# Two-layer streaming encoder step on one core: norm tiles, key transposes and a residual addition issued at other places

## Chip, cores and metric

One NeuronCore of a Trainium2 chip runs the whole program in one launch. The time is device microseconds of that core; the figure compared is the median over executions.

## What is computed

A step of a two-layer encoder in fp32 for 512 prompt tokens and 8 x 16 sample tokens, together 640 tokens in T = 5 tiles of 128. Each layer is mixer, cross-attention into 256 memory tokens, gated MLP, each behind an RMSNorm and followed by a residual addition:

```python
for l in range(2):
    x = x + mixer_l(rmsnorm(x, ln_mix[l]))        # l=0: attention + retention, l=1: gated linear attention
    mn = rmsnorm(mem, ln_mem[l])                  # 256 memory tokens of the prompt
    k, v = mn @ w_ck[l], mn @ w_cv[l]             # sample tokens use cached k, v, one pair per sequence
    x = x + softmax((rmsnorm(x, ln_cross[l]) @ w_cq[l]) k^T / 16) v @ w_co[l]
    x = x + conv_ffn(rmsnorm(x, ln_ffn[l]))       # gelu(conv(h Wg)) * (h Wu) @ Wdown
y = rmsnorm(x, ln_final)
```

The model width is 1024, cross-attention has 4 heads of 256. New keys, values and states are outputs too.

## The kernel before, in words

**Products.** Every large product is split into high and low fp32r parts and made of three matmuls a slice of 128 contraction rows: high x low, low x high, high x high (`three`, L784 to L788). Weights come in units of 1024 columns: SyncE loads them into `raw`, ScalarE copies out the high part (`split_hi`, L1530), VectorE subtracts to get the low part (`split_lo`, L2056). There are 5 slots for split units; ScalarE may fill one only when TensorE has marked it free, and TensorE waits for the low part. A product of one token tile by 512 columns is 8 slices, 24 matmuls of 512 columns (`proj_tile`, `proj_out`). A product with the weights standing (`cols_tile`) has two parts of 384 and 256 tokens; `cols_pair` does two such column tiles for the first three token tiles, and then both for the last two.

**Norm tiles.** For tile t of a norm, ScalarE squares and sums (L1575), GpSimd makes the reciprocal root (L535, L536), VectorE scales into `xn` (`scaled`, L2073; two buffers), TensorE transposes in two halves of four 128x128 blocks (`norm_tile`, L801 to L810), ScalarE copies the high part of each half (`halves`, L1591) and VectorE makes the low part (`halves`, L2090), which also drains the bank. These transposes, the key transposes and the scores share 3 PSUM banks in turn (`aux`); product outputs share the other 5 (`lin`). A bank can be opened again only when what was in it is drained.

**Order.** The order of each engine's work is written out by hand; every engine works its own list strictly in order and waits on semaphores. `norm_behind` (L1132) runs the last product of a stage tile by tile with the norm's transposes behind it. Its last two tiles, T-2 and T-1, are transposed inside the first product of the next chunk: `cols_pair` calls them before slice 0 and slice 3 of its second column tile (L1139).

**The parts that the change touches.** `rest(l)` holds the cross-attention and MLP of layer l, on each engine. On TensorE: query chunk `("cq", l, 0)` ends with column tiles 2 and 3, with both memory norm tiles transposed between them (L1145 to L1147); the four tiles of `("cq", l, 1)`; then the two key chunks, each of two products (memory tiles m = 0, 1), and after both products the transposes of both results (`mkT`, L1152 to L1158), for which ScalarE must have copied the product out to `mk` (L1780). VectorE copies each `mkT` block out (L2378). Then 4 of 8 slices of a value product, a wait for the last `mkT` copy, and eight score steps (`x_scores`). After the prompt's attention come NB + 3 = 11 stages s for the 8 sample sequences (L1215 to L1270): in each, part of an output product `("co", l, 0)` (`CROSS_FILL`, L186: tile 0 in stages 1 and 2, tile 1 in 3 and 4, tile 2 in 6 and 7, tile 3 in 8 and 9), transposes of the cached keys (L1227) whose copies to `kTX` ScalarE (L1814) and VectorE (L2403) share, transposes of the probabilities of sequence s - 2 (L1234), scores of sequence s - 1 (L1253), values of s - 2 (L1264). VectorE adds a finished output tile to x with `add_x` (L2104), which also drains the product's bank; in a stage it does so last (L2421).

In the MLP's down products (`down`, L2430 on VectorE) each token tile has two halves n of 512 columns. In the last group of layer 0 (`behind`) VectorE interleaves the additions with `scaled` and `halves` of norm `mix1`, and splits unit 0 of the next chunk `("in1", 0)` ahead of the addition (t, n) = (1, 0) (L2438).

Of the kernel before, what the change touches and what calls it, by code (L numbers as in the profile page):

```python
# [19 lines left out]
P = 128  # L20
D = 1024
KT = D // P
# [3 lines left out]
T = TP + 1  # L26
# [175 lines left out]
def build(nc, io, known):  # L202
# [8 lines left out]
    with ctx:  # L211
# [571 lines left out]
        def _(pe):  # L783
# [345 lines left out]
                        ins.then_inc(*unit_free.mark(c, k // 2))  # L1129
                ins.then_inc(*lin_full.mark(c, t))  # L1130

            def norm_behind(nm, product, following):  # L1132

                for t in range(T):
                    product(t)
                    if 0 < t < T - 1:
                        norm_tile(nm, t - 1)

                cols_pair(nm, following, 0, {(1, 0): lambda: norm_tile(nm, T - 2), (1, 3): lambda: norm_tile(nm, T - 1)})  # L1139
                cols_pair(nm, following, 1)  # L1140


            def rest(l):
                c = ("cq", l, 0)
                cols_tile(c, f"cross{l}", P * 2, 2)  # L1145
                norm(f"mem{l}")
                cols_tile(c, f"cross{l}", P * 3, 3, last=True)  # L1147
                for i in range(4):
                    cols_tile(("cq", l, 1), f"cross{l}", P * i, i, last=i == 3)
                for c in (("ck", l, 0), ("ck", l, 1)):  # L1150
                    proj_rows(c, f"mem{l}", 2, memT_lo, memT_hi)
                    for m in range(2):  # L1152
                        pe.wait_ge(*act_done.at("mk", l, m, c[2]))
                        out = aux.open(pe, "mkT", l, c[2], m)
                        for i in range(4):
                            k = 4 * c[2] + i
                            ins = pe.transpose(out[:, P * i:P * i + P], mk[:, m, P * k:P * k + P], ident[:, :])
                        ins.then_inc(*aux_full.mark("mkT", l, c[2], m))  # L1158

                pe.wait_ge(*act_done.at("cq", l, 1, 3))  # L1160
                pairs = [(t, hp) for t in range(TP) for hp in range(2)]

                def x_scores(t, hp):
                    out = aux.open(pe, "sX", l, t, hp)
                    for hh in range(2):
                        for dk in range(2):
                            k = 4 * hp + 2 * hh + dk
                            ins = pe.matmul(out[:, MEM * hh:MEM * hh + MEM], qT[:, t, k, :], mkT[:, k, :], start=dk == 0, stop=dk == 1)  # L1168
                    ins.then_inc(*aux_full.mark("sX", l, t, hp))
# [13 lines left out]
                        ins.then_inc(*lin_full.mark(c, m))  # L1183

                value_part(0, 0, 0)
                pe.wait_ge(*dve_done.at("mkT", l, 1, 1))
                x_scores(0, 0)
                for n, (t, hp) in enumerate(pairs):
                    if n + 1 < len(pairs):
# [130 lines left out]
                        ins = pe.transpose(out[0:18, P * (f - 4 * n):P * (f - 4 * n) + P], tailc[:, f, :], ident[:, :])  # L1320
                    ins.then_inc(*aux_full.mark("rows", l, n))
                if l == 0:
                    norm_behind("mix1", lambda t: down(GROUPS - 1, t), [(("in1", 0), 0, 0), (("in1", 0), P, 1)])
                else:
                    for t in range(T):
                        down(GROUPS - 1, t)
# [179 lines left out]
        def _(act):  # L1506
# [253 lines left out]
            def rest(l):  # L1760
                for half in range(2):
                    c = ("cq", l, half)
                    for i in range(4):
                        if i == 1:
                            split_hi(NEXT[c], [0])
                        if i == 3:
                            split_hi(NEXT[c], [1, 2, 3])
                        k = 4 * half + i
                        evac_cols(c, i, qT[:, :, k, :], 1.0, ("cq", l, half, i))
                        if half == 0 and i == 1:  # L1770
                            norm(f"mem{l}", "mem")

                def memory(name, half, m):

# [260 lines left out]
        def _(dve):  # L2035
# [332 lines left out]

            def rest(l):
                split_lo(NEXT[("cq", l, 0)], [0])  # L2370
                norm(f"mem{l}")
                split_lo(NEXT[("cq", l, 0)], [1, 2, 3])
                split_lo(NEXT[("cq", l, 1)], range(4))
                for half in range(2):
                    split_lo(NEXT[("ck", l, half)], range(4))
# [21 lines left out]
                for s in range(NB + 3):  # L2397
                    if s == 0:
                        dve.wait_ge(*put["mv"].at(l))
                    if s < NB:  # L2400
                        for n in (1, 3):
                            dve.wait_ge(*aux_full.at("kTX", l, s, n))
                            dve.tensor_copy(kTX[s % 2][:, 2 * n:2 * n + 2, :], aux.bank("kTX", l, s, n)[:, :].rearrange("p (k m) -> p k m", k=2)).then_inc(*aux_v.mark("kTX", l, s, n))  # L2403
                            dve_done.after("kTX", l, s, n)
                    if 1 <= s <= NB:
                        b, i = s - 1, (s - 1) % 2
                        dve.wait_ge(*aux_full.at("sXs", l, b))
                        link(dve.tensor_reduce(small[:, i, 0:1], aux.bank("sXs", l, b)[:, 0:MEM], AX.X, ALU.max))
                        dve.tensor_scalar(small[:, i, 1:2], small[:, i, 0:1], -1.0 / 16.0, None, ALU.mult).then_inc(*dve_done.mark("negXs", l, b))
                        dve.wait_ge(*aux_a.at("sXs", l, b))  # L2410
                        link(dve.reciprocal(small[:, i, 3:4], small[:, i, 2:3]))
                        dve.tensor_scalar(pS[:, i, :], pS[:, i, :], small[:, i, 3:4], lam_mask[:, i:i + 1], ALU.mult, ALU.mult).then_inc(*dve_done.mark("pS", l, b))
                    if s >= 4 and s % 2 == 0:
                        p = s // 2 - 2
                        dve.wait_ge(*act_done.at("oX", l, p))
                        cols = slice(SEQ + 32 * p, SEQ + 32 * p + 32)
                        dve.tensor_tensor(hT_lo[:, :, cols].rearrange("p (h j) q -> p h j q", j=2), lin.bank("oXT", l, p)[:, 0:2 * P].rearrange("p (j h q) -> p h j q", j=2, h=H),
                                          flat(hT_hi[:, :, cols]).rearrange("p (h j) q -> p h j q", j=2), ALU.subtract).then_inc(*lin_v.mark("oXT", l, p))
                    if s == NB:
                        split_lo(("co", l, 1), [0])  # L2420
                    if s in CROSS_FILL and CROSS_FILL[s][2] == KT:  # L2421
                        add_x(("co", l, 0), CROSS_FILL[s][0], 0)
                    if s == NB + 1:
                        add_x(("co", l, 0), TP - 1, 0)
                dve_done.after("oX", l)
# [4 lines left out]
                def down(g):  # L2430
# [4 lines left out]
                    for t in range(T):  # L2435
                        for n in range(2):
                            if c in NEXT:
                                if t == 1 and n == 0:  # L2438
                                    split_lo(NEXT[c], [0])
                                if t == T - 1 and n == (1 if behind else 0):  # L2440
                                    split_lo(NEXT[c], [1, 2, 3])
# [4 lines left out]
                            if behind and t and n == 0:  # L2446

                                if t < T - 1:
                                    scaled(nm, t - 1)
                                if t > 1:  # L2450
                                    halves(nm, t - 2)
                    if behind:
                        scaled(nm, T - 2)
                        scaled(nm, T - 1)
# [270 lines left out]
```

## Time and profile before

| | us |
|---|---|
| median of 3 runs | 2092.57 |
| lowest and highest of them | 2091.99, 2093.45 |
| the profiled execution | 2091.57 |
| its span in the trace | 2089.8 |
| TensorE busy, share of the span | 98% |
| VectorE / ScalarE / GpSimd busy | 47% / 36% / 10% |

The span runs from the first to the last instruction of the profiled execution; its own time is 1.8 us longer. A timeline line reads: start in us, duration in us, engine (PE TensorE, DVE VectorE, ACT ScalarE, POOL GpSimd, SP SyncE), line of the kernel, operation, out<-in by the program's names, shapes, count; in brackets the idle time of the engine before it and what ended that. Lines with a count merge instructions that follow one another.

### The profile page before, as it was taken

How to read it: one execution, taken by the hardware profiler on the slowest of the kernel's cores; microseconds unless marked ns; L12 is line 12 of the kernel's file. 1: busy time of each engine (PE TensorE's matmuls, PEld its weight loads, DVE VectorE, ACT ScalarE, POOL GpSimd, SP SyncE). 2: the span in 40 equal slices, each digit the busy share in tenths (PEclk: the TensorE clock that was granted, in tenths of full speed). 3: DMA queues.
4: the chain of work that ended last, by engine and by line, in shares of the span. 5: the costliest groups of instructions: out<-in, count | busy, mean ns of one | idle time of the engine just before them, and what ended most of it. 6: DMA issues, size and time to landing. Idle time of an engine off the chain costs nothing.

```text
span 2089.8 us, 30525 instructions
## 1 busy us (share of the span) xinstructions
PE 2040.5 (98%) x12370; PEld 1795.0 (86%) x12370; DVE 981.9 (47%) x1651; ACT 762.3 (36%) x1318; POOL 199.1 (10%) x457
## 2 busy tenths in 40 slices
PE   8999989999999999999999999999999999999997
PEld 6889667987789999999989888799778999999996
DVE  5453664435454443434453467653444444434443
ACT  4222552435344332232233446243533433223232
POOL 3012121000100000000010123210010000000000
PEclk9999999999999999999999999999999999999999
DMA  5324143235722222222221211723572132122221
GB/s 164 132 77 149 51 160 128 85 121 198 262 84 77 66 81 81 69 76 68 81 77 61 81 44 43 257 71 121 184 290 85 62 100 80 63 70 81 81 81 55
DMA packets 111066, 219.42 MB, mean 105 GB/s; under 512 B 7011, under 2 KB 52367, under 8 KB 110862
## 3 DMA queue, kind: packets, MB, share of 16 engines
q1 hardware_dynamic: 91234, 148.00, 20.8%
q0 software_dynamic: 19696, 69.47, 9.7%
q8 instruction: 102, 1.67, 0.3%
q14 instruction: 34, 0.28, 0.0%
HBM read 200.51 MB, written 18.24 MB: 105 GB/s over the span
## 4 chain that ended last, share of the span: by engine, by line
PE 93%; DVE 3%; ACT 2%; issue 1%; DMA 1%; POOL 0%; DVEq 0%; SPq 0%; ACTq 0%; POOLq 0%
PE bank L786 15%; PE bank L788 14%; PE bank L787 14%; PE bank L847 7%; PE bank L851 7%; PE bank L849 7%; PE bank L850 5%; PE bank L848 5%; PE bank L852 5%; PE bank L809 1%; PE bank L1211 1%; PE bank L1227 1%; PE bank L1168 1%; PE bank L1253 1%; PE bank L1264 1%
## 5 line engine op out<-in xcount | busy, mean ns | idle before, releaser
L2056 DVE TENSOR_TENSOR w_lo<-raw,w_hi 128x1024 fp32r<-128x1024 f32 x265 | 319.0, 1219 | 524.2 <-ACT w_hi L1530 520.3
L1530 ACT ACTIVATE w_hi<-raw 128x1024 fp32r<-128x1024 f32 x265 | 274.4, 1052 | 252.3 <-PE bank L788 202.4
L786 PE MATMUL bank<-w_hi,hT_lo 128*128 128x512 f32 x720 | 291.3, 405 | 10.4 <-DVE x L2104 4.3
L847 PE MATMUL bank<-hT_hi,w_lo 128*128 128x384 f32 (+1 forms) x856 | 290.0, 339 | 0.0
L849 PE MATMUL bank<-hT_lo,w_hi 128*128 128x384 f32 (+1 forms) x856 | 289.3, 338 | 0.0
L851 PE MATMUL bank<-hT_hi,w_hi 128*128 128x384 f32 (+1 forms) x856 | 289.3, 338 | 0.0
L788 PE MATMUL bank<-w_hi,hT_hi 128*128 128x512 f32 x720 | 282.7, 393 | 0.0
L787 PE MATMUL bank<-w_lo,hT_hi 128*128 128x512 f32 x720 | 282.1, 392 | 0.0
L848 PE MATMUL bank<-hT_hi,w_lo 128*128 128x256 f32 (+1 forms) x856 | 239.0, 279 | 0.0
L850 PE MATMUL bank<-hT_lo,w_hi 128*128 128x256 f32 (+1 forms) x856 | 239.0, 279 | 0.0
L852 PE MATMUL bank<-hT_hi,w_hi 128*128 128x256 f32 (+1 forms) x856 | 239.0, 279 | 0.0
L786 PEld LDWEIGHTS bank<-w_hi,hT_lo 128*128 128x128 f32 x720 | 136.1, 189 | 50.5 <-issue 9.4
L2104 DVE TENSOR_TENSOR x<-x,bank 128x512 f32<-128x512 f32 x160 | 109.5, 685 | 145.4 <-PE bank L788 144.6
L786 PE MATMUL bank<-w_hi,a_lo 128*128 128x512 f32 x440 | 171.7, 390 | 0.0
L788 PE MATMUL bank<-w_hi,a_hi 128*128 128x512 f32 x440 | 171.2, 389 | 0.0
L787 PE MATMUL bank<-w_lo,a_hi 128*128 128x512 f32 x440 | 171.2, 389 | 0.0
L847 PEld LDWEIGHTS bank<-hT_hi,w_lo 128*128 128x128 f32 (+1 forms) x856 | 160.0, 187 | 1.9 <-DVE memT_lo L2090 0.4
L788 PEld LDWEIGHTS bank<-w_hi,hT_hi 128*128 128x128 f32 x720 | 136.0, 189 | 29.6
L851 PEld LDWEIGHTS bank<-hT_hi,w_hi 128*128 128x128 f32 (+1 forms) x856 | 160.0, 187 | 0.6
L849 PEld LDWEIGHTS bank<-hT_lo,w_hi 128*128 128x128 f32 (+1 forms) x856 | 160.0, 187 | 0.6
L848 PEld LDWEIGHTS bank<-hT_hi,w_lo 128*128 128x128 f32 (+1 forms) x856 | 160.1, 187 | 0.5
L850 PEld LDWEIGHTS bank<-hT_lo,w_hi 128*128 128x128 f32 (+1 forms) x856 | 160.1, 187 | 0.2
(368 smaller groups left out, 2990.7 us busy)
## 6 DMA issues: line engine op xcount, KB each, us to landing
raw<-w_ffn_gate SPq DMA_DIRECT2D x44, 512.0 KB, 3.8
raw<-w_ffn_up SPq DMA_DIRECT2D x44, 512.0 KB, 4.8
raw<-w_ffn_down SPq DMA_DIRECT2D x22, 1024.0 KB, 4.8
kcX<-cache_mem_k POOLq DMA_DIRECT2D x16, 1024.0 KB, 6.6
vcX<-cache_mem_v POOLq DMA_DIRECT2D x16, 1024.0 KB, 6.9
raw<-w_in_even SPq DMA_DIRECT2D x13, 1024.0 KB, 5.3
raw<-w_in_odd SPq DMA_DIRECT2D x12, 1024.0 KB, 5.1
raw<-w_cq SPq DMA_DIRECT2D x8, 1024.0 KB, 7.3
```

What stands on the lines that cost most here:

```text
L786: pe.matmul(out, wl, xh, start=first, stop=False)
L787: pe.matmul(out, wh, xl, start=False, stop=False)
L788: return pe.matmul(out, wh, xh, start=False, stop=last)
L847: pe.matmul(oa, wl, hT_hi[:, k, 0:HA], start=f, stop=False)
L848: pe.matmul(ob, wl, hT_hi[:, k, HA:TOK], start=f, stop=False)
L849: pe.matmul(oa, wh, hT_lo[:, k, 0:HA], start=False, stop=False)
L850: pe.matmul(ob, wh, hT_lo[:, k, HA:TOK], start=False, stop=False)
L851: ia = pe.matmul(oa, wh, hT_hi[:, k, 0:HA], start=False, stop=l)
L852: ib = pe.matmul(ob, wh, hT_hi[:, k, HA:TOK], start=False, stop=l)
L1530: act.activation(w_hi[:, g % W_SLOTS, 0:n], raw[:, q % 2, UNIT * i:UNIT * i + n], ACT.Copy).then_inc(*hi_made.mark(c, u))
L2056: dve.tensor_tensor(w_lo[:, s, 0:n], raw[:, q % 2, UNIT * i:UNIT * i + n], flat(w_hi[:, s, 0:n]), ALU.subtract).then_inc(*lo_made.mark(c, u))
L2104: ins = dve.tensor_tensor(xs, xs, lin.bank(c, t, *key)[:, :], ALU.add)
```

## The change

All edits are of order; every transpose, product, copy, split and addition is there before and after, and one wait moves.

- `mix1` only: tiles T-2 and T-1 are transposed before slices 2 and 4 of the second column tile, not 0 and 3. On VectorE the split of unit 0 of `("in1", 0)` moves from before the addition (1, 0) to behind the addition (1, 1).
- The memory norm's tile 0 is transposed between query column tiles 2 and 3, tile 1 after tile 3. ScalarE makes the second tile's high part, and VectorE its low part, that much later, behind the splits of the next units.
- The key transposes go one by one: (half 0, m 0) before slice 6 of the product (0, 1), (0, 1) inside product (1, 0), (1, 0) inside product (1, 1), and (1, 1) after the first half of the value product. The score steps of token tile 0 wait for the copy of their own half's second block.
- In the stages that end an output tile (2, 4 and 7) VectorE adds it first, before the key copies.

```diff
 # TensorE
-            def norm_behind(nm, product, following):
+            def norm_behind(nm, product, following, turns=(0, 3)):
...
-                cols_pair(nm, following, 0, {(1, 0): lambda: norm_tile(nm, T - 2), (1, 3): lambda: norm_tile(nm, T - 1)})
+                cols_pair(nm, following, 0, {(1, turns[0]): lambda: norm_tile(nm, T - 2), (1, turns[1]): lambda: norm_tile(nm, T - 1)})
...
-                norm(f"mem{l}")
+                norm_tile(f"mem{l}", 0)
                 cols_tile(c, f"cross{l}", P * 3, 3, last=True)
+                norm_tile(f"mem{l}", 1)
...
-                for c in (("ck", l, 0), ("ck", l, 1)):
-                    proj_rows(c, f"mem{l}", 2, memT_lo, memT_hi)
-                    for m in range(2):
...
+                proj_tile(("ck", l, 0), f"mem{l}", 0, 2, memT_lo, memT_hi)
+                proj_tile(("ck", l, 0), f"mem{l}", 1, 2, memT_lo, memT_hi, lambda: turn_keys(0, 0))
+                proj_tile(("ck", l, 1), f"mem{l}", 0, 2, memT_lo, memT_hi, lambda: turn_keys(0, 1))
+                proj_tile(("ck", l, 1), f"mem{l}", 1, 2, memT_lo, memT_hi, lambda: turn_keys(1, 0))
...
                 def x_scores(t, hp):
+                    if t == 0:
+                        pe.wait_ge(*dve_done.at("mkT", l, hp, 1))
...
                 value_part(0, 0, 0)
-                pe.wait_ge(*dve_done.at("mkT", l, 1, 1))
+                turn_keys(1, 1)
                 x_scores(0, 0)
...
-                    norm_behind("mix1", lambda t: down(GROUPS - 1, t), [(("in1", 0), 0, 0), (("in1", 0), P, 1)])
+                    norm_behind("mix1", lambda t: down(GROUPS - 1, t), [(("in1", 0), 0, 0), (("in1", 0), P, 1)], (2, 4))
 # ScalarE
                         if half == 0 and i == 1:
-                            norm(f"mem{l}", "mem")
+                            square(f"mem{l}", "mem", 0)
+                            square(f"mem{l}", "mem", 1)
+                            halves(f"mem{l}", 0)
+                        if half == 0 and i == 3:
+                            halves(f"mem{l}", 1)
 # VectorE
                 split_lo(NEXT[("cq", l, 0)], [0])
-                norm(f"mem{l}")
+                scaled(f"mem{l}", 0)
+                scaled(f"mem{l}", 1)
+                halves(f"mem{l}", 0)
                 split_lo(NEXT[("cq", l, 0)], [1, 2, 3])
+                halves(f"mem{l}", 1)
...
                 for s in range(NB + 3):
                     if s == 0:
                         dve.wait_ge(*put["mv"].at(l))
+                    if s in CROSS_FILL and CROSS_FILL[s][2] == KT:
+                        add_x(("co", l, 0), CROSS_FILL[s][0], 0)
...
-                    if s in CROSS_FILL and CROSS_FILL[s][2] == KT:
-                        add_x(("co", l, 0), CROSS_FILL[s][0], 0)
...
-                                if t == 1 and n == 0:
+                                if t == 1 and n == 0 and not behind:
                                     split_lo(NEXT[c], [0])
...
+                            if behind and (t, n) == (1, 1):
+                                split_lo(NEXT[c], [0])
```

## Rows read from the trace of the kernel before

**Rows 1.** The page: busy time by engine, share of the span, instructions

```profile
PE 2040.5 (98%) x12370; PEld 1795.0 (86%) x12370; DVE 981.9 (47%) x1651; ACT 762.3 (36%) x1318; POOL 199.1 (10%) x457
```

**Rows 2.** Who waited for whom, TensorE: us in total, times, longest us

```profile
PE bank L786 <- DVE x L2104: 4.3, 3, 1.9
...
PE bank L809 <- DVE memT_lo L2090: 1.1, 2, 0.5
```

**Rows 3.** Timeline, down products of layer 0, first transposes of norm mix1

```profile
1062.34 1.23 DVE L2056 TENSOR_TENSOR w_lo<-raw,w_hi 128x1024 fp32r<-128x1024 f32 x1 [2.24 <-ACT w_hi L1530]
...
1064.20 1.28 DVE L2073 SCALAR_TENSOR_TENSOR xn<-x,rstd,gain 128x1024 f32<-128x1024 f32 x1
...
1064.36 0.39 PE L788 MATMUL bank<-w_hi,a_hi 128*128 128x512 f32 x1
...
1065.54 0.66 PE L809 MATMUL bank<-ident,xn 128*128 128x128 f32 x4 [0.79 <-DVE xn L2073]
```

**Rows 4.** Timeline, column pair behind it, tiles T-2 and T-1 of norm mix1

```profile
1088.76 0.34 PE L788 MATMUL bank<-hT_hi,w_hi 128*128 128x384 f32 x1
1089.78 1.06 PE L809 MATMUL bank<-ident,xn 128*128 128x128 f32 x8 [0.68 <-DVE xn L2073]
...
1090.33 1.29 DVE L2073 SCALAR_TENSOR_TENSOR xn<-x,rstd,gain 128x1024 f32<-128x1024 f32 x1 [0.81 <-POOL rstd L536]
...
1092.27 1.03 PE L809 MATMUL bank<-ident,xn 128*128 128x128 f32 x8
...
1093.53 1.29 DVE L2090 TENSOR_TENSOR hT_lo<-bank,hT_hi 128x512 fp32r<-128x512 f32 x2 [0.72 <-ACT hT_hi L1591]
```

**Rows 5.** Timeline, a norm tile without a wait, then the two memory tiles, layer 0

```profile
384.70 1.04 PE L809 MATMUL bank<-ident,xn 128*128 128x128 f32 x8
...
385.50 0.42 PE L786 MATMUL bank<-hT_hi,w_lo 128*128 128x384 f32 x1
...
403.80 1.47 PE L809 MATMUL bank<-ident,xn 128*128 128x128 f32 x12
...
406.44 0.41 PE L847 MATMUL bank<-hT_hi,w_lo 128*128 128x384 f32 x1
```

**Rows 6.** Timeline, TensorE, first block of key transposes of layer 0

```profile
452.63 0.60 PE L1157 MATMUL bank<-ident,mk 128*128 128x128 f32 x4
...
453.89 0.47 PE L786 MATMUL bank<-w_hi,memT_lo 128*128 128x512 f32 x1
454.20 0.39 PE L787 MATMUL bank<-w_lo,memT_hi 128*128 128x512 f32 x1
454.43 0.39 PE L788 MATMUL bank<-w_hi,memT_hi 128*128 128x512 f32 x1
```

**Rows 7.** Timeline, key transposes to scores, stages 3 and 5, layer 0

```profile
536.88 1.94 PE L1227 MATMUL bank<-ident,kcX 128*128 128x128 f32 x16
...
538.97 1.07 PE L1253 MATMUL bank<-kTX,qT 128*32 128x256 f32 x16
...
547.87 2.00 PE L1227 MATMUL bank<-ident,kcX 128*128 128x128 f32 x16
...
549.45 0.67 DVE L2104 TENSOR_TENSOR x<-x,bank 128x512 f32<-128x512 f32 x1
...
550.99 1.07 PE L1253 MATMUL bank<-kTX,qT 128*32 128x256 f32 x16 [0.32 <-DVE kTX L2403]
```

**Rows 8.** Timeline, stage 7 and the product of stage 8, layer 0; last, layer 1

```profile
562.78 1.94 PE L1227 MATMUL bank<-ident,kcX 128*128 128x128 f32 x16
...
563.86 0.69 DVE L2403 COPY kTX<-bank 128x512 f32<-128x512 f32 x1 [2.39 <-PE bank L1227]
...
568.72 0.50 PE L786 MATMUL bank<-w_hi,hT_lo 128*128 128x512 f32 x1 [1.91 <-DVE x L2104]
...
1567.26 0.50 PE L786 MATMUL bank<-w_hi,hT_lo 128*128 128x512 f32 x1 [1.78 <-DVE x L2104]
```

**Rows 9.** Stretches: length, busy of PE PEld DVE ACT POOL, granted clock, DMA share, GB/s

```profile
519.00:552.00 33.00, 32.29 (x288) 24.52 (x290) 16.81 (x34) 12.02 (x27) 6.42 (x9) 1.00 0.85 312
```

More of the change, by code:

```diff
@@ L1145, in rest, with turn_keys @@
                 cols_tile(c, f"cross{l}", P * 2, 2)
-                norm(f"mem{l}")
+                norm_tile(f"mem{l}", 0)
                 cols_tile(c, f"cross{l}", P * 3, 3, last=True)
+                norm_tile(f"mem{l}", 1)
                 for i in range(4):
                     cols_tile(("cq", l, 1), f"cross{l}", P * i, i, last=i == 3)
-                for c in (("ck", l, 0), ("ck", l, 1)):
-                    proj_rows(c, f"mem{l}", 2, memT_lo, memT_hi)
-                    for m in range(2):
[L1153 to L1158, printed above, removed]
+                def turn_keys(half, m):
+                    pe.wait_ge(*act_done.at("mk", l, m, half))
+                    out = aux.open(pe, "mkT", l, half, m)
+                    for i in range(4):
+                        k = 4 * half + i
+                        ins = pe.transpose(out[:, P * i:P * i + P], mk[:, m, P * k:P * k + P], ident[:, :])
+                    ins.then_inc(*aux_full.mark("mkT", l, half, m))
+                proj_tile(("ck", l, 0), f"mem{l}", 0, 2, memT_lo, memT_hi)
+                proj_tile(("ck", l, 0), f"mem{l}", 1, 2, memT_lo, memT_hi, lambda: turn_keys(0, 0))
+                proj_tile(("ck", l, 1), f"mem{l}", 0, 2, memT_lo, memT_hi, lambda: turn_keys(0, 1))
+                proj_tile(("ck", l, 1), f"mem{l}", 1, 2, memT_lo, memT_hi, lambda: turn_keys(1, 0))
                 pe.wait_ge(*act_done.at("cq", l, 1, 3))
```

## The prediction

> **What bounds the kernel now.** I read the page first, then the list of who waited for whom, then the timeline around each wait of TensorE, and last the stretch table for the clock. The page [rows 1] has TensorE busy in 2040.5 of 2089.8 us: VectorE, the next, is busy 47% of the span and the weight loads run beside the matmuls, so only a TensorE gap is worth anything, and all its gaps together are 49.3 us. The change moves instructions only, so it can win or lose only in gaps. The wait list [rows 2] names those that this change touches: product openings waiting for a residual addition on VectorE (4.3 us in 3 times) and transposes of normalised tiles waiting for their bank. The timeline shows each gap's place, and there I read starts, not the idle column: a 512-wide matmul lasts 0.39 us but the next starts 0.23 us after it [rows 6], so a gap is the start that came less the start that was due. The idle column leaves out the drain of the pipe and comes out smaller.
>
> **Part A, the mixing norm of layer 1 (once).** Product 1 of the last down group has its last matmul at 1064.36; the transposes were due 0.23 later, at 1064.59, and started at 1065.54: a gap of 0.95 us [rows 3]. They waited for the scaled tile (1064.20 to 1065.48), which stands on VectorE behind a weight split of 1.23 us (1062.34). The change puts that split behind the two additions of this tile. The addition could have started about when the split did: its half product is 12 matmuls before 1064.36, so starts its last matmul at 1061.6 and is through at 1062.0. The scaled tile then ends some 1.2 us earlier, at about 1064.3, before 1064.59. Gain 0.95. The split's weights are needed only after three more down products (24 matmuls of 0.23 each, 5.5 us), so its delay of about 3 us is hidden behind those; without that cover it would cost its 1.23.
>
> The turn of tile T-2 now sits at slice 0 of the second column product. Due at 1088.93, it came at 1089.78: 0.85 us [rows 4]. From that turn to the next (1092.27) there are 0.80 for 8 transposes, 0.09 for the return, and 9 matmuls, so a matmul takes 0.175 and a slice of three 0.53. At slice 2 the turn is due at 1089.98, after 1089.78, when it was free to go: gain 0.85. Tile T-1 moves from slice 3 to 4 and comes due at 1089.98 + 0.89 + 1.06 = 1091.93; its scaled tile ends at 1091.62 (1090.33 + 1.29), the margin is 0.3. Its second half needs the bank that VectorE drains for T-2 only after that scaled tile, at about 1091.62 + 0.64 = 1092.3, just when TensorE wants it (1091.93 + 0.40): I charge 0.1. What is late next: the low parts of T-1 ended at 1094.82, 2.55 after its turn; now 1094.48, and the second half of the columns opens at 1091.93 + 0.89 + 4 x 0.53 = 1094.9. It fits by 0.4. Part A: 0.95 + 0.85 - 0.1 = **1.7 us**.
>
> **Part B, memory norm tiles (both layers).** The two tiles were turned in a row: 16 transposes from 403.80 to the next product at 406.44, 2.64 us. One tile's 8 transposes with nothing to wait for take 385.50 - 384.70 = 0.80 [rows 5]. The difference is the fourth bank of a set of three, which had to be drained first, 1.1 us of idle time in both layers together [rows 2]. With a product of some 7 us between the tiles (24 matmuls of 384 columns at 0.175 and 24 of 256 at two thirds of it) the bank is long empty: 2 x 0.80. Added is one more return from transposes to a product. After a turn the second matmul starts 0.31 after the first, not 0.23 [rows 6], which is 0.08, with the next few 0.09. So 2.64 - 1.60 - 0.09 = 0.95 a layer, **1.9 us**. ScalarE and VectorE now do the second tile's high and low parts behind the splits of the next chunk; first needed by the key products, four such products later, they are hidden behind those 28 us.
>
> At this return the Trainium skill says otherwise: "TensorE: Matmul & The Clock Gate", the section on what happens when a matmul is issued, has the engine's reorder window pull weight loads ahead of matmuls in flight, which would make a return free. Rows 6 speak against it, 0.31 against 0.23. By that rule the sum below would be 0.5 us larger (six returns of 0.09, an estimate).
>
> **Part C, key transposes (both layers).** Each of the two blocks a layer takes 1.26 us (452.63 to 453.89) for 8 transposes, because the second tile's keys are only now being copied out by ScalarE [rows 6]. After the change there are four blocks of half the length, 0.40 each by rows 5, three of them at slice 6 of the product that follows, some 4 us after the copy could start, and the last behind half a value product (12 matmuls, 2.7 us). Two more returns: 2.52 - 1.60 - 0.18 = 0.74 a layer; I take 0.7, **1.4 us**. Behind the moved turns on their queues: VectorE now stands before the copy of block 2 until slice 6 of the next product, with the split of the value weights behind it. Its first unit is needed only after one more key product of 5.4 us, and the slots of the others come free only in that product. GpSimd's store of the keys waits for ScalarE, not for the turns; only its next load, of cached keys, waits for the last turn and comes 3 us later, with all eight score steps ahead of its use. The change adds one wait: the first score step of the second head pair waits for the last block's copy on VectorE, 0.69 as in rows 8, and all of TensorE's stream is queued behind it. Its cover is the first score step, four fp32 matmuls of 256 columns, of which no row here gives the pace; at no less than the 0.23 of rows 6 they take 0.9, longer than the copy. I take 0, the other bound is 0.7 a layer.
>
> **Part D, the addition ahead of the key copies (both layers).** Before, the addition for a finished output tile stood at the end of the stage on VectorE. Two places pay for it. In stage 5, which has no product to hide under, it runs at 549.45 and pushes back the key copies; scores start 550.99 - 547.87 = 3.12 us after the key transposes, against 538.97 - 536.88 = 2.09 in a stage without it [rows 7]. The copies start 0.7 earlier without it (its 0.67 and a gap), so 0.7 of this 1.03 goes and 0.3 stays: 1.4 in both layers. In stage 8 the product needs the very bank that the addition of tile 2 drains: idle 1.91 and 1.78 us [rows 8]. The new place is right after the product, at about 562.9: 5 us before. Gain 3.7. Does the moved addition now push key copies in its own stage? Product through at about 562.94 (last start 0.23 before 562.78, duration 0.39), a lag to the next engine that is 0.06 in rows 3 and that I put at 0.15, addition 0.67: 563.76. The copy that follows starts at 563.86. It fits by 0.1, so 0; the bound is the whole 0.67 each, three times a layer. Part D: 1.4 + 3.7 = **5.1 us**.
>
> **Sum.** 1.7 + 1.9 + 1.4 + 5.1 = 10.1 us. SyncE's weight loads wait for splits that wait for TensorE's slots, so they move along. The profiled execution took 2091.57, which becomes 2081.5. The median of the runs is 1.0 above it, so for the median 2092.57 - 10.1 = **2082.5**.
>
> **Rivals.**
> 1. The woven turns give nothing (B and C): a turn in the middle of an accumulation breaks the stream by more than 0.09, or a wait of equal size takes the place. For it: rows 6 show that a return has a price, and I have it from one kind of product. Against: rows 4 have turns inside a product, at 0.89 in all. Time: 2092.57 - 6.8 = 2085.8.
> 2. The addition holds up the key copies, since it fits by only 0.1 [rows 8]. Six times 0.67, 4.0 us back: 2086.5. Against: in the stages of rows 7 and 8 VectorE idles before the copy (2.39 in rows 8), so nothing else is in the way.
> 3. The freed waits are passed on, above all stage 8's: the next thing that TensorE wants there is the transposed probabilities. Then A brings half, 0.9, and D nothing; with B and C that is 4.2 us or less: 2088.4 or more, no change. Against: VectorE made those probabilities before the addition of rows 8, so they are there when TensorE comes.
> 4. Slower: the clock. In the stretch with the most transposes of all the granted clock is 1.00, the level of 2.4 GHz [rows 9], with products on either side. If the engine's clock fell to 1.2 GHz where transposes now cut into the key products, each of their 24 matmuls would take twice its 0.23: 5.4 us more a product, three products a layer, 33 us in all, 2115. It decides from the point where 14 us of matmuls run at half. The Trainium skill has the ground for this: the same page, in its part on the transpose, says that the transposes don't count as activity for the clock in the way that matmuls do. Rows 9 speak against it here.
>
> **How the numbers follow.** Forecast 0.76, rival 1 0.08, rival 2 0.07, rival 3 0.05, rival 4 0.02, and 0.02 for a wait that I haven't seen. About 0.2% (4 us) is what a measurement of this kernel can tell from no change, so faster means under 2088.4: the forecast and the first two, and a little of the rest: 0.93; same 0.05; slower 0.02. The range goes up to rival 2, 2086.5. Down it takes in free returns (0.5), the rest of stage 5's wait (0.6) and the 0.1 and rounding: 2080.9.
>
> **What the profile would show.** No wait of TensorE on the residual addition in stages 5 and 8 of both cross attentions, 0.3 or so left on the key copy of stage 5; no wait of transposes on a memory tile's low part, none on keys being copied out, and neither of the gaps of rows 3 and 4. Part D carries half: if 1.9 us of idle time stand before the stage 8 product, under whatever name, the forecast is wrong by 3.7. A new wait of TensorE before the second score step would show that part C's last turn comes too late, and a clock under 1.00 in the key stretch would be rival 4.

## The result, and the profile after

The changed kernel takes 2081.39 us (median of 6 runs, 2080.77 to 2082.18) against 2092.98 for the kernel before in the same session (2091.71 to 2093.51): ratio 0.9946, 95% interval 0.9936 to 0.9957. The forecast was 2082.5, the range 2080.9 to 2086.5. Timed again in another session, the two stood at 2081.06 and 2092.08, ratio 0.9945 (0.9932 to 0.9957). So the change wins 11.0 to 11.6 us by the medians where 10.1 were forecast. The intervals of the two ratios reach from 9 to 14 us, so the medians alone couldn't tell 10.1 from 11.6; the comparison of the traces below can.

The page of the changed kernel, busy time by engine, answers to [rows 1]:

```profile
PE 2038.8 (98%) x12370; PEld 1795.5 (86%) x12370; DVE 983.1 (47%) x1651; ACT 761.9 (37%) x1318; POOL 198.8 (10%) x457
```

TensorE does the same work in a span of 2080.3 us in place of 2089.8; the idle time went from 49.3 to 41.5 us, 7.8 of the 9.5 us. The rest is in the busy time: a product's last matmul is listed with 0.39 us where the next is due after 0.23, so about 0.16 of each closed gap had counted as busy (an estimate; ten such gaps make 1.6). The list of who waited for whom (us in total, times, longest us) answers to [rows 2]:

```profile
PE bank L996 <- DVE sA L2317: 4.8, 3, 3.1
...
PE bank L809 <- DVE xn L2084: 2.1, 1, 2.1
...
PE bank L786 <- DVE x L2115: 0.6, 1, 0.6
...
PE bank L1260 <- DVE kTX L2419: 0.2, 1, 0.2
```

The wait of products on the residual addition fell from 4.3 us in 3 times to 0.6 in 1; those of the transposes on a memory tile's low part (1.1 us) and on keys being copied out (1.0 us before) are gone from the list; the 2.1 us on a scaled tile are those of the first norm of the kernel, which nothing touched. The wait on top was there before too (4.9 us in 3 times), elsewhere in the kernel.

The timeline of the changed kernel, at the four places of the change. Part A, the down products and the column pair, answers to [rows 3, 4]:

```profile
1059.61 1.28 DVE L2084 SCALAR_TENSOR_TENSOR xn<-x,rstd,gain 128x1024 f32<-128x1024 f32 x1
...
1061.11 0.39 PE L788 MATMUL bank<-w_hi,a_hi 128*128 128x512 f32 x1
1061.34 1.03 PE L809 MATMUL bank<-ident,xn 128*128 128x128 f32 x8
...
1062.26 1.22 DVE L2067 TENSOR_TENSOR w_lo<-raw,w_hi 128x1024 fp32r<-128x1024 f32 x1
...
1085.74 1.03 PE L809 MATMUL bank<-ident,xn 128*128 128x128 f32 x8
...
1086.09 1.28 DVE L2084 SCALAR_TENSOR_TENSOR xn<-x,rstd,gain 128x1024 f32<-128x1024 f32 x1 [0.81 <-POOL rstd L536]
...
1087.66 1.03 PE L809 MATMUL bank<-ident,xn 128*128 128x128 f32 x8
...
1088.93 1.29 DVE L2101 TENSOR_TENSOR hT_lo<-bank,hT_hi 128x512 fp32r<-128x512 f32 x2 [0.35 <-ACT hT_hi L1598]
```

The split (1062.26) now stands behind the scaled tile (1059.61), and the transposes follow the last matmul by 0.23 us: no gap. In the column pair the wait of the first turn is gone, and the second has none, as before.

Parts B and C, the second memory tile, the first woven block of key transposes and the last block of the layer, answer to [rows 5, 6] (PEld is TensorE's weight load):

```profile
413.02 1.03 PE L809 MATMUL bank<-ident,xn 128*128 128x128 f32 x8
413.81 0.42 PE L847 MATMUL bank<-hT_hi,w_lo 128*128 128x384 f32 x1
...
451.37 0.39 PE L788 MATMUL bank<-w_hi,memT_hi 128*128 128x512 f32 x1
...
451.61 0.60 PE L1157 MATMUL bank<-ident,mk 128*128 128x128 f32 x4
...
451.96 0.48 PE L786 MATMUL bank<-w_hi,memT_lo 128*128 128x512 f32 x1
452.04 0.19 PEld L787 LDWEIGHTS bank<-w_lo,memT_hi 128*128 128x128 f32 x1
452.27 0.40 PE L787 MATMUL bank<-w_lo,memT_hi 128*128 128x512 f32 x1
452.27 0.19 PEld L788 LDWEIGHTS bank<-w_hi,memT_hi 128*128 128x128 f32 x1
452.51 0.40 PE L788 MATMUL bank<-w_hi,memT_hi 128*128 128x512 f32 x1
...
452.74 0.40 PE L786 MATMUL bank<-w_hi,memT_lo 128*128 128x512 f32 x1
...
468.02 0.60 PE L1157 MATMUL bank<-ident,mk 128*128 128x128 f32 x4
...
468.46 3.62 PE L1175 MATMUL bank<-mkT,qT 128*128 128x256 f32 x16
```

A memory tile takes 0.79 us from its first transpose to the product, as the tile without a wait did. A block of four key transposes takes 0.35 until the product goes on, and the return after it is again 0.31 in place of 0.23. The weight loads show where the 0.08 lies: the load for the second matmul starts at 452.04, 0.08 behind the first matmul, where the next load starts together with the matmul ahead of it (both 452.27). The last block (468.02) holds up the first score step by 0.44.

Part D, stage 5 and stages 7 and 8 of the first cross attention, answers to [rows 7, 8]:

```profile
547.34 2.00 PE L1234 MATMUL bank<-ident,kcX 128*128 128x128 f32 x16
...
548.92 1.27 DVE L2419 COPY kTX<-bank 128x512 f32<-128x512 f32 x2
...
561.76 0.69 DVE L2115 TENSOR_TENSOR x<-x,bank 128x512 f32<-128x512 f32 x1 [1.56 <-PE bank L788]
...
562.70 1.53 DVE L2419 COPY kTX<-bank 128x512 f32<-128x512 f32 x2 [0.26 <-PE bank L1234]
...
565.51 0.50 PE L786 MATMUL bank<-w_hi,hT_lo 128*128 128x512 f32 x1
```

The addition runs at 561.76, ahead of the copies, and the product of stage 8 (565.51) has no wait. In stage 5 the copies start 1.58 us after the key transposes (2.28 before), and the scores there start at 549.74, 2.40 after them in place of 3.12.

To see how much each place brought, take matmuls before and behind it and set the start of each against that of the same matmul in the trace before; the step in the difference is what the place won. Which matmuls are taken moves a step by up to 0.07 us. In us, for the trace shown above and for that of the kernel's second session:

```
part, layer               forecast   first trace   second trace
B, memory tiles, 0          0.95        0.98          0.97
C, key transposes, 0        0.70        0.81          0.82
D, stage 5, 0               0.70        0.79          0.74
D, stage 8, 0               1.91        1.94          2.00
A, down products            0.95        0.99          1.00
A, column pair              0.75        0.86          0.82
B, 1                        0.95        0.99          0.99
C, 1                        0.70        0.87          0.87
D, stage 5, 1               0.70        0.82          0.74
D, stage 8, 1               1.78        1.88          1.87
sum                        10.1        10.9          10.8
```

The two profiled executions shown above differ by only 9.4 us (2091.57 and 2082.18). The rest is a stretch that the change doesn't touch: at 300 to 310 us the granted clock was 0.83 in the trace after and 1.00 in the trace before, and by the same comparison the second trace of the changed kernel is 1.2 us shorter from there on. The last experiment comes back to such stretches.

### The profile page after: what moved, and what is told of

It is laid out like the page before. It is cut to its first block, busy times and chain, and to the rows that moved or that the text cites. A ratio compares the mean times of both kernels' runs of the same rounds, so it can differ in the third digit from the quotient of the medians.

```text
span 2080.3 us, 30527 instructions
## 1 busy us (share of the span) xinstructions
PE 2038.8 (98%) x12370; PEld 1795.5 (86%) x12370; DVE 983.1 (47%) x1651; ACT 761.9 (37%) x1318; POOL 198.8 (10%) x457
## 4 chain that ended last, share of the span: by engine, by line
PE 94%; DVE 2%; ACT 2%; issue 1%; DMA 1%; POOL 0%; DVEq 0%; SPq 0%; ACTq 0%; POOLq 0%
PE bank L786 15%; PE bank L788 15%; PE bank L787 15%; PE bank L847 7%; PE bank L851 7%; PE bank L849 7%; PE bank L848 5%; PE bank L852 5%; PE bank L850 5%; PE bank L809 1%; PE bank L1218 1%; PE bank L1234 1%; PE bank L1175 1%; PE bank L1260 1%; PE bank L1271 1%
```

## The experiments

Theory 1 is the prediction's own: every part is a TensorE gap of known size, the parts don't touch each other, and a saved microsecond stays saved. Against it stand that waits are passed on from one part to the next (rival 3), that the moved addition costs the key copies something (rival 2), and that a return from transposes is either free or dearer than 0.09.

Enough executions for an interval were made of d_only, abc_only, late7, mixc_early and, twice, of the changed kernel. The others were executed once each, under the profiler, and are read by the steps of their one trace: a_split 2091.80 us, a_turns 2092.77, late4 2082.41, keys_single 2082.62, add_two 2082.03, add_three 2085.57. So a_split and a_turns show no gain against the 2092.26 and 2092.57 of the kernel before: each lost more to a lower clock at 570 us than it won at the changed place (experiment 6).

**1. Part D alone and parts A to C alone.**

```diff
 # d_only: the kernel before with
+                    if s in CROSS_FILL and CROSS_FILL[s][2] == KT:
+                        add_x(("co", l, 0), CROSS_FILL[s][0], 0)
                     if s < NB:
                         for n in (1, 3):
...
-                    if s in CROSS_FILL and CROSS_FILL[s][2] == KT:
-                        add_x(("co", l, 0), CROSS_FILL[s][0], 0)
 # abc_only: the changed kernel with the same four lines put back
```

> The kernel before with part D alone: the residual addition ahead of the key copies, norms and key turns as they were. My theory: D is worth 2 x 0.75 in stage 5 and 1.9 + 1.8 in stage 8, 5.2 us, by itself, and the other gaps stay as before (0.95 and 0.85 in the mixing norm, 1.1 of waits on memT_lo, two key blocks of 1.26 a layer): ratio 0.9975. Theory 'the parts feed each other' (a gap closed by one part lets the other gain): D alone gives 4 us or less, or 6.5 or more. Rival 2 of the prediction (the addition holds up key copies): 1.2 us.

> The changed kernel with part D undone: the residual addition stands at the end of the stage again. My theory: A, B and C keep their 1.9 + 1.85 + 1.7 = 5.5 us against before (ratio 0.9974), and the waits of TensorE on the addition come back with 1.9 and 1.8 us before the products of stage 8 and 0.7 in each stage 5. 'The parts feed each other': the sum of this run's gain and that of part D alone differs from the gain of both by over 1.5 us.

Measured: D alone 2086.80 against 2092.26, ratio 0.9970 (0.9960 to 0.9981); A to C alone 2087.63, ratio 0.9974 (0.9964 to 0.9984). In the traces D alone steps by 0.72, 1.99, 0.76 and 1.88, together 5.35 us, and A to C alone by 0.97, 0.80, 1.01, 0.86, 0.98 and 0.88, together 5.50. Their sum is 10.85, against 10.8 for both together. The medians agree less well, 5.5 us for D and 4.6 for A to C, 10.1 in all, but each of these has an uncertainty of about 2 us. By the traces nothing is passed on and nothing feeds another part: rival 3 falls. The waits of TensorE on the addition, first of A to C alone, where the stage 8 gaps are back, then of D alone, where they are gone:

```profile
PE bank L786 <- DVE x L2115: 4.3, 3, 1.9
```

```profile
PE bank L786 <- DVE x L2104: 0.6, 1, 0.6
```

**2. Part D, one stage undone at a time.**

```diff
 # late7; late4 has 4 for 7
-                    if s in CROSS_FILL and CROSS_FILL[s][2] == KT:
+                    if s in CROSS_FILL and CROSS_FILL[s][2] == KT and s != 7:
                         add_x(("co", l, 0), CROSS_FILL[s][0], 0)
...
+                    if s in CROSS_FILL and CROSS_FILL[s][2] == KT and s == 7:
+                        add_x(("co", l, 0), CROSS_FILL[s][0], 0)
```

> The changed kernel with part D undone in stage 7 alone. My theory: the gap before the stage 8 product comes back in both layers, 1.9 + 1.8 = 3.7 us over the changed kernel, the rest of D stays. Beside it a second theory, formed after the first runs: two traces of kernels with this gap (the two halves of part A alone) showed a granted clock of 0.83 to 0.87 at 570 to 580 us, right behind it, worth some 1.7 us, and none of the traces without it did. If the gap is what sets this off, runs of this kernel spread over 3 us or more from the lowest to the highest, with the median over 3.7 above the changed kernel's. If such stretches come by chance, the spread is that of the changed kernel, 2 us or less.

> The changed kernel with part D undone in stage 4 alone. My theory: only stage 5 loses, 0.75 us a layer, 1.5 over the changed kernel's trace, under the waits on the addition and the key copies; stage 8 has no gap. Theory 'both gaps of D hang on one thing': stage 8 or later stages move too.

Measured: late4 lost 0.71 and 0.69 us at stage 5 and nothing at stage 8. With late7 the first layer lost 1.97 at stage 8 and nothing at stage 5; the second lost 3.41, 1.85 of it ahead of the product and 1.56 just behind its start, of which more in experiment 6. Each half of D hangs on its own addition; the third moved addition, that of stage 2, had no step in the trace of d_only.

**3. The two halves of part A.** a_split moves only VectorE's weight split behind the second tile's additions; a_turns moves only the two turns.

```diff
 # a_split: the kernel before with
-                                if t == 1 and n == 0:
+                                if t == 1 and n == 0 and not behind:
                                     split_lo(NEXT[c], [0])
...
+                            if behind and (t, n) == (1, 1):
+                                split_lo(NEXT[c], [0])
 # a_turns: the kernel before with
-                cols_pair(nm, following, 0, {(1, 0): ..., (1, 3): ...})
+                cols_pair(nm, following, 0, {(1, 2 if nm == "mix1" else 0): ..., (1, 4 if nm == "mix1" else 3): ...})
```

> The kernel before with one thing of part A alone: in the last down group of layer 0 the weight split of VectorE stands behind the two additions of tile 1, the turns in the column pair stay at slices 0 and 3. My theory: the first gap (0.95 us, down products) is gone; the second, 0.85 us at the first turn in the column pair, stays whole, since the scaled tile it waits for hangs on the last down product, which moves along: -0.95 us from there on. Rival 'the wait is passed on': TensorE arrives 0.95 earlier at a tile made at the same time, the second gap grows to 1.8 and the two together give 0.

> The kernel before with the other half of part A alone: the two last turns of the mixing norm at slices 2 and 4 of the second column product instead of 0 and 3; VectorE's order as before. My theory: the first gap (0.95 us, in the down products) stays, the second (0.85) goes, and the bank for the second half of tile T-1 costs up to 0.1: -0.75 to -0.85 us from there on. Rival 'the later low parts': the second half of the columns opens late and gives back 0.4 or more.

Measured: a_split won 1.01 in the down products and 0.00 in the column pair; a_turns won 0.00 and 0.83. The timelines of a_split, then of a_turns, show the gap that each one left:

```profile
1065.39 0.39 PE L788 MATMUL bank<-w_hi,a_hi 128*128 128x512 f32 x1
...
1065.62 1.03 PE L809 MATMUL bank<-ident,xn 128*128 128x128 f32 x8
...
1088.78 0.34 PE L788 MATMUL bank<-hT_hi,w_hi 128*128 128x384 f32 x1
...
1089.80 1.07 PE L809 MATMUL bank<-ident,xn 128*128 128x128 f32 x8 [0.69 <-DVE xn L2073]
```

```profile
1064.17 1.23 DVE L2056 TENSOR_TENSOR w_lo<-raw,w_hi 128x1024 fp32r<-128x1024 f32 x1 [2.24 <-ACT w_hi L1530]
...
1066.03 1.28 DVE L2073 SCALAR_TENSOR_TENSOR xn<-x,rstd,gain 128x1024 f32<-128x1024 f32 x1
...
1067.37 1.09 PE L809 MATMUL bank<-ident,xn 128*128 128x128 f32 x8 [0.79 <-DVE xn L2073]
```

In a_turns the first gap is whole (the last matmul starts at 1066.19, so 1067.37 is 0.95 late). In a_split the second gap is 1.02 less the 0.175 of a matmul, 0.85 as before, though TensorE came a microsecond earlier: the tile that it waits for hangs on TensorE's own last down product and moved along. A gap whose releaser is made from TensorE's latest output isn't enlarged by arriving earlier. The rival would have been right for a tile made from something else.

**4. The price of a woven transpose.** Each woven key block is taken apart into four single transposes:

```diff
 # keys_single: the changed kernel; turn_keys(half, m, i) issues transpose i alone
-                    if between and k == 6:
-                        between()
+                    if between and what.startswith("mem") and 3 <= k < 7:
+                        between(k - 3)
+                    elif between and k == 6:
+                        between()
```

> The changed kernel with each of the three woven key blocks of a layer taken apart: its four transposes one by one ahead of slices 3, 4, 5 and 6 of the key product, so 3 more returns from a transpose to a matmul a block, 18 in all. My theory: a return costs 0.08 to 0.09 us, so each of those three products lasts 0.25 longer and the kernel 1.5 us more than the changed one. By the rule of the Trainium skill (page 'TensorE: Matmul & The Clock Gate', what happens when a matmul is issued) weight loads are pulled ahead and the returns are free: 0.0 us. The clock rival: more switching between kinds lowers the granted clock in this stretch; expected 1.00.

Measured: 0.15 us more in the first layer and 0.13 in the second, 0.28 for 18 more returns. Neither theory. The timeline of this kernel shows why:

```profile
449.53 0.39 PE L788 MATMUL bank<-w_hi,memT_hi 128*128 128x512 f32 x1
449.76 0.27 PE L1160 MATMUL bank<-ident,mk 128*128 128x128 f32 x1
449.79 0.48 PE L786 MATMUL bank<-w_hi,memT_lo 128*128 128x512 f32 x1
450.10 0.39 PE L787 MATMUL bank<-w_lo,memT_hi 128*128 128x512 f32 x1
450.33 0.39 PE L788 MATMUL bank<-w_hi,memT_hi 128*128 128x512 f32 x1
450.56 0.27 PE L1160 MATMUL bank<-ident,mk 128*128 128x128 f32 x1
```

The return does cost 0.08 (0.31 from 449.79 to 450.10, not 0.23), each time. By the rule of the Trainium skill ("TensorE: Matmul & The Clock Gate", what happens when a matmul is issued) weight loads are pulled ahead of matmuls in flight, from which I had drawn that a return would be free; here it isn't. But the product's matmul starts only 0.03 behind a single transpose, while four in a row hold it up by 0.35. From transpose to transpose a slice takes 0.80, and three matmuls take 0.68: a single transpose costs 0.12 with its return. A block of four costs 1.13 (451.61 to 452.74) less 0.68, 0.45, or 0.11 each. The first transpose after a matmul is nearly hidden, and what it saves pays for the return. Woven transposes cost 0.11 to 0.12 us each, one by one or four in a row.

**5. How much room the moved addition had.**

```diff
 # add_two: the changed kernel with extra=1 for the moved additions; add_three: extra=2
                 xs = x[:, t, 512 * n:512 * n + 512]
+                for _ in range(extra):
+                    dve.tensor_tensor(xn[:, _, 0:512], xs, lin.bank(c, t, *key)[:, :], ALU.add)
```

> The changed kernel with the moved addition's cost doubled: one more VectorE operation of the same shape (x plus the product's bank, into a scratch tile) ahead of each moved addition, in stages 2, 4 and 7 of both cross attentions. Nothing else differs. My theory of the margin, by the changed kernel's trace: the scores need the bank that the first key copy of VectorE empties; they start 0.19 (stage 2), 0.48 (stage 4) and 0.30 (stage 7) after its end, of which 0.14 is the lag, so 0.69 more on VectorE comes out as 0.6 + 0.35 + 0.5 of waiting a layer: 2.9 us over the changed kernel, under the name of the key copy. Rival 'there is room' (VectorE is only 47% busy): 0. Rival 'no margin at all': 6 x 0.69 = 4.1.

> The same with two more operations ahead of each moved addition. With the margins used up by the first, the second should come out whole: 2.9 + 6 x 0.69 = 7.0 us over the changed kernel. Rival 'the loss saturates', since the work of TensorE ahead of the scores hides more: 4 or less.

Measured by the same comparison: add_two 1.1 us over the changed kernel (2.9 expected), add_three 4.6 (7.0 expected). VectorE in stage 4, of add_two and then of add_three, with the scores of the latter:

```profile
542.58 0.69 DVE L2116 TENSOR_TENSOR xn<-x,bank 128x512 f32<-128x512 f32 x1 [1.86 <-PE bank L788]
543.18 0.68 DVE L2117 TENSOR_TENSOR x<-x,bank 128x512 f32<-128x512 f32 x1
...
543.90 1.29 DVE L2421 COPY kTX<-bank 128x512 f32<-128x512 f32 x2
```

```profile
545.02 1.29 DVE L2421 COPY kTX<-bank 128x512 f32<-128x512 f32 x2
...
545.85 1.07 PE L1260 MATMUL bank<-kTX,qT 128*32 128x256 f32 x16 [0.58 <-DVE kTX L2421]
```

Two things were missing from my expectation. The extra operation of 0.69 us is followed by the next after 0.60 (542.58 to 543.18); behind the addition into x the next one starts only after 0.72 (543.18 to 543.90). And the copy of the changed kernel had stood idle for 0.25 or 0.26 on the transposes in stages 2, 4 and 7 (562.70 above), which an operation ahead of it partly fills for nothing. With both, the copies start 1.32 behind the first operation (542.58 to 543.90) where they started 0.94 behind the addition (561.76 to 562.70): the first extra one delays them by 0.38. Less the slack that the expectation gives (0.05 in stage 2, 0.34 in stage 4, 0.16 in stage 7) that is 0.33, 0.04 and 0.22; the measured steps are 0.28, 0 and 0.28 in the first layer, 0.25, 0 and 0.32 in the second. The second one costs 3.5 in six places, 0.59 each on average, so in full. So there was room for the addition and about a third of another: rival 2 was wrong, but one more operation there is paid for, though VectorE is 47% busy.

**6. The clock behind a gap.** The second layer of late7, its timeline on TensorE:

```profile
1560.49 0.50 PE L786 MATMUL bank<-w_hi,hT_lo 128*128 128x512 f32 x1 [1.79 <-DVE x L2115]
1560.83 0.39 PE L787 MATMUL bank<-w_lo,hT_hi 128*128 128x512 f32 x1
1561.06 0.39 PE L788 MATMUL bank<-w_hi,hT_hi 128*128 128x512 f32 x1
...
1561.82 0.63 PE L788 MATMUL bank<-w_hi,hT_hi 128*128 128x512 f32 x1
1562.25 0.63 PE L786 MATMUL bank<-w_hi,hT_lo 128*128 128x512 f32 x1
1562.68 0.63 PE L787 MATMUL bank<-w_lo,hT_hi 128*128 128x512 f32 x1
```

A microsecond behind the gap the starts go from 0.23 to 0.43 apart: the clock fell from 2.4 to 1.2 GHz. The table of stretches (length, busy time of PE, PEld, DVE, ACT and POOL, granted clock, DMA share, GB/s) has it too; here late7, then a_turns, then the kernel before:

```profile
1560.00:1570.00 10.00, 9.51 (x61) 6.87 (x62) 3.05 (x7) 2.24 (x6) 0.00 (x0) 0.83 0.31 107
```

```profile
570.00:580.00 10.00, 10.00 (x75) 6.59 (x73) 3.40 (x7) 2.56 (x6) 0.00 (x0) 0.83 0.23 93
```

```profile
570.00:580.00 10.00, 9.49 (x81) 6.37 (x80) 3.69 (x8) 3.33 (x8) 0.00 (x0) 1.00 0.19 79
```

It costs 3.41 - 1.85 = 1.56 us in late7, and a_split and a_turns lose 1.55 and 1.57 at 570 us. It doesn't come every time. Five traces have the stage 8 gap in both layers (before, A to C alone, both halves of A, late7): of these 10 gaps 3 are followed by such a stretch. Eight traces have no such gap, and in their 16 places there is none. If three such stretches fell by chance on any of the 26 places, all three would be among those 10 in one case of 22, and two of the three are those that gave me the theory. The last run compared the spread:

> The changed kernel once more, timed together with the one above: ratio to before 0.9945 +- 0.001. With no gap before the stage 8 product, by the clock theory no granted clock under 0.9 at 570 to 580 us, and runs within 2 us of each other; by chance alone, as wide as the other.

Measured: the changed kernel 2080.37 to 2081.22 in 5 runs, 0.85 wide; late7 2084.13 to 2087.40 in 6, 3.3 wide, its median 4.4 above, where the gaps alone are 3.82 (1.97 + 1.85); the kernel before, ten runs beside them, 2091.38 to 2094.63. Both criteria came out as the theory that the gap sets it off has it. But the spread has another source too: the stretch at 300 us alone moves a run by 1.2 us. And the runs of experiment 1 don't tell the two theories apart: A to C alone, with both gaps, is 2.1 wide in 8 runs, D alone, without them, 1.9 in 8. With 3 of 10 against 0 of 16 I call it likely, not shown; what decides whether a given gap is followed by it stays open.

**7. One more order of the same kind.**

```diff
 # mixc_early: the changed kernel
+            mixed_turn(1, 3)
             read_state(0)
             read_state(1)
-            mixed_turn(1, 3)
...
-            gla_sq(act, 0, TP)
             mixed_hi("mixC", 3, 1)
+            gla_sq(act, 0, TP)
```

> The changed kernel with one more order of its kind, in layer 1 behind the recurrence: TensorE turns the mixed tile of chunk 3 ahead of the state reads of heads 0 and 1 instead of behind them, and ScalarE copies it out ahead of its square. The turn then stands some 3.1 us earlier and the product that waits for its low part (gap 1.33 us at 1318 us) finds it there. My theory: 1.3 us less than the changed kernel in the trace (ratio to before 0.994). Rival 'VectorE has no time for the low part before the next addition': no gain. Rival 'passed on': the next state write, which waits for banks that VectorE empties, takes it back.

Measured: 2079.78 us (2079.16 to 2080.89), ratio 0.9937 (0.9924 to 0.9951), and a step of 1.46 us in the trace, where the idle column had said 1.33 and the drain of the pipe comes on top. The turn stands at 1310.38, its low part is through by 1312.4, and the product at 1315.05 has no wait. It is faster than both kernels, by 1.3 to 1.6 us against the changed one by the medians and by 1.46 by the trace; the medians alone couldn't tell that.

## Why the prediction was right

Each step held, and every place came within 0.2 us of its term. All the differences lie on one side, and added up they are the 0.7 to 0.8 us by which the traces exceed the forecast.

- **What bounds the kernel.** Only gaps of TensorE count, and starts tell their size. The steps in the table agree with the gaps read that way within 0.12 for A, B and D. For stage 8 I had broken my own rule and taken the idle column, 1.91 and 1.78; the steps are 0.03 to 0.10 larger.
- **Part A.** 0.99 and 0.86 for 0.95 and 0.75. The 0.1 charged for the bank of tile T-1's second half wasn't paid: VectorE began draining tile T-2 at 1087.29 (the whole tile takes it 1.28), right behind the scaled tile; TensorE wanted the bank 0.40 behind 1087.66, at 1088.06, and the turn shows no wait.
- **Part B.** 0.98 for 0.95. The turn of 0.79 and the return of 0.08 to 0.09 were both right.
- **Part C.** The term that was furthest off: 0.81 and 0.87 for 0.70. I put a block at 0.40 and its return at 0.09, 0.49 in all. A key product with a woven block lasts 5.92 us and one without 5.46, so a block costs 0.46 with its return, and the fourth, in front of the scores, costs about the same (0.44). That is 0.12 less for the four than I put. From the first key product to the first score step the kernel before takes 27.25 us (441.72 to 468.97) and the changed one 26.41 (442.05 to 468.46): 0.84 less, and the table has 0.81 to 0.87. I had also rounded 0.74 down to 0.70. The added wait before the second score step didn't show.
- **Part D.** 0.79 and 1.94, 0.82 and 1.88 for 0.70 and 1.91, 0.70 and 1.78. The residue in stage 5 is there and as I put it, 0.3: the scores come 2.40 behind the key transposes (547.34 to 549.74), where 2.09 was the free value. Read so, stage 5 wins 0.72, and the table, from matmuls farther apart, has 0.74 to 0.82.
- **Rivals.** 1 fell by the steps of B and C, 2 by experiment 5 (the copy at 562.70 waited 0.26 for the transposes, not for the addition: I had seen 0.1 of room), 3 by experiment 1. Rival 4, a clock lowered by the woven transposes, has no trace: the key stretch had no granted clock under 1.00 in any profile, keys_single among them. Where the clock does fall, it is behind a wait.
- **Sum.** 10.1 forecast, 10.9 and 10.8 in the traces, 11.0 and 11.6 by the medians. What the medians have beyond the traces lies within their uncertainty; if it is real, experiment 6 has a candidate: the gaps of stage 8 in the kernel before cost their 3.7 us and in 3 cases of 10 another 1.56, about 0.9 a run. The forecast priced a gap at its length only. No run shows this extra gain: D alone takes both gaps away too, and its median gained 5.5 us where its trace gained 5.35.

## What to carry over

On a kernel whose TensorE is 98% busy, list every wait of it, take each gap as a difference of starts, and ask of each which instruction on the releaser's queue could stand elsewhere. Such orders added up here: ten gaps of 0.7 to 2 us gave 10.8, part by part and without loss. Before putting an operation ahead of another on a queue that looks half idle, read the idle time right before the one it delays; that and the time by which the delayed result comes early, not the busy share, are the room.

## What the runs showed of the hardware that I had not expected

- A single transpose between fp32 product matmuls costs 0.12 us, and four in a row 0.45: the 0.08 of each return is made good by the 0.03 that the first transpose takes in place of 0.11.
- VectorE's 128x512 operations with an operand in PSUM last 0.69 us by the trace. The extra additions into a scratch tile and the key copies are followed by the next every 0.60, the additions into x only after 0.72; what makes the difference no run shows.
- TensorE's clock can fall to 1.2 GHz about 1 us behind a wait of 1.8 to 1.9 us in an otherwise full stretch; it did so behind 3 of 10 such waits and cost 1.55 to 1.57 us each time. That the wait sets it off is likely, not shown.
